# One long fp32 kernel: values and gates of each head pair as one 512-column product, input on the weights' queue, unread products at three waits, token scaling on GpSimd

## The reference, cut to what matters

```
# h_lat, h_ctx: 256 tokens each x 2048; 16 heads of 128
zf, zb, i, q, g = split(h_lat @ w_in, 5 x 2048)        # latent tokens: all five
zf_c, zb_c, i_c = split(h_ctx @ w_in[:, :6144], 3)     # context tokens: three
for each direction (forward with zf, backward with zb):
    f = lb + (1 - lb) * sigmoid(z);  k = (1 - lb) * sigmoid(-z)
    s_ctx = final state of k_c, v_c over the context, by chunks
    o    += chunked scan S_t = f_t S_(t-1) + k_t v_t, o_t = S_t q_t, from s_ctx
o = o * rsqrt(mean(o * o over 128) + eps)              # per token and head
y = (o * onorm_g * g * sigmoid(g)) @ w_out
```

## Time and profile before

| what | value |
| --- | --- |
| median of 3 runs | 3124.61 us |
| the profiled execution | 3124.67 us, of which the profile's span is 3122.9 |
| TensorE busy | 3083.2 us, 99% |
| VectorE, ScalarE, GpSimd busy | 64%, 46%, 3% |
| moved | 557.59 MB, mean 179 GB/s |
| one head pair of the recurrent mixer | some 99.7 us, eight of them |

### The profile page before, as it was taken

The page is one execution under the profiler, slowest core; times in us unless marked ns, Lnnn a source line. Parts: engine busy times, 40 slices in busy tenths (PEclk is TensorE's granted clock), DMA queues, the critical chain, the costliest instruction groups (busy, mean ns, idle before and its releaser), DMA issues.

```text
span 3122.9 us, 41500 instructions
## 1 busy us (share of the span) xinstructions
PE 3083.2 (99%) x16978; PEld 2666.3 (85%) x16978; DVE 1998.3 (64%) x2502; ACT 1422.3 (46%) x2029; POOL 97.3 (3%) x74
## 2 busy tenths in 40 slices
PE   8999999999999999999999999999999999999998
PEld 8989888888888888878888888888889999899987
DVE  6767777789888887857877755442743444443455
ACT  5344555465555554436422222232644544444454
POOL 0000003001111100000000000000000000000000
PEclk9999999999999999999999999999999999999999
DMA  8776666757667677775556555342333333333334
GB/s 302 231 248 216 208 212 216 250 179 230 213 221 225 216 251 266 254 240 197 161 170 191 178 193 179 127 150 95 103 96 104 100 108 114 102 110 97 112 131 146
DMA packets 369982, 557.59 MB, mean 179 GB/s; under 512 B 17088, under 2 KB 239296, under 8 KB 368512
## 3 DMA queue, kind: packets, MB, share of 16 engines
q1 hardware_dynamic: 366784, 540.08, 53.6%
q0 software_dynamic: 2000, 12.06, 1.0%
q10 hardware_dynamic: 1008, 2.80, 0.2%
HBM read 552.64 MB, written 2.23 MB: 178 GB/s over the span
## 4 chain that ended last, share of the span: by engine, by line
PE 95%; DVE 2%; ACT 1%; issue 1%; DMA 1%; ACTq 0%; DVEq 0%
PE ps L736 91%; DVE wlo L1746 1%; PE ps L933 0%; PE ps L948 0%; PE ps L938 0%; PE ps L950 0%; ACT whi L1152 0%; PE ps L807 0%; DMA CX<-in_ctx 0%; PE ps L771 0%; DVE HCl L1900 0%; PE ps L861 0%; PE ps L845 0%; PE ps L918 0%; PE ps L935 0%
## 5 line engine op out<-in xcount | busy, mean ns | idle before, releaser
L1746 DVE TENSOR_TENSOR wlo<-raw,whi 128x1024 fp32r<-128x1024 f32 (+1 forms) x823 | 1013.4, 1235 | 822.5 <-ACT whi L1152 820.6
L1152 ACT ACTIVATE whi<-raw 128x1024 fp32r<-128x1024 f32 x828 | 869.9, 1057 | 1166.5 <-PE ps L736 1150.3
L736 PE MATMUL ps<-HCh,whi 128*128 128x512 f32 (+1 forms) x1816 | 508.2, 361 | 0.0
L736 PE MATMUL ps<-HCh,wlo 128*128 128x512 f32 (+1 forms) x1816 | 500.8, 357 | 0.0
L736 PE MATMUL ps<-HCl,whi 128*128 128x512 f32 (+1 forms) x1816 | 500.3, 357 | 0.0
L736 PE MATMUL ps<-V,whi 128*128 128x512 f32 x1408 | 445.2, 398 | 0.8 <-DVE V L1902 0.8
L1763 DVE SCALAR_TENSOR_TENSOR acc<-raw_ada,S,acc 128x1024 f32<-128x1024 f32 x330 | 436.4, 1334 | 5.0 <-DMA raw_ada<-in_ada_w 4.2
L736 PEld LDWEIGHTS ps<-HCh,wlo 128*128 128x128 f32 x1816 | 323.6, 189 | 49.8
L736 PEld LDWEIGHTS ps<-HCl,whi 128*128 128x128 f32 x1816 | 323.5, 189 | 49.8
L736 PEld LDWEIGHTS ps<-HCh,whi 128*128 128x128 f32 x1816 | 319.7, 190 | 49.7 <-issue 4.2
L736 PEld LDWEIGHTS ps<-V,wlo 128*128 128x128 f32 x1408 | 265.4, 188 | 62.8
(11 more groups left out here) (345 smaller groups left out, 3484.5 us busy)
## 6 DMA issues: line engine op xcount, KB each, us to landing
raw_ada<-in_ada_w SPq DMA_DIRECT2D x192, 512.0 KB, 4.8
raw<-in_w_up SPq DMA_DIRECT2D x176, 512.0 KB, 4.3
raw<-in_w_in SPq DMA_DIRECT2D x160, 512.0 KB, 4.0
raw<-in_od_w_in SPq DMA_DIRECT2D x160, 512.0 KB, 3.5
raw<-in_ev_w_in SPq DMA_DIRECT2D x96, 512.0 KB, 3.8
raw<-in_w_down SPq DMA_DIRECT2D x88, 512.0 KB, 5.1
raw<-in_w_out SPq DMA_DIRECT2D x32, 512.0 KB, 4.8
raw<-in_w_ple_gate SPq DMA_DIRECT2D x32, 512.0 KB, 4.6
```

What stands on the lines that cost most here:

```text
L736: mm = e.matmul(o, a, b, start=first and t == 0, stop=last, skip_group_check=True)
L1152: e.activation(m.whi[ch.i % SPLIT][:, 0:n], m.raw[ch.slot][:, 0:n], ACT.Copy).then_inc(S("hi"), 1)
L1746: e.tensor_tensor(m.wlo[ch.i % SPLIT][:, 0:n], m.raw[ch.slot][:, 0:n], m.whi[ch.i % SPLIT][:, 0:n].bitcast(F32), ALU.subtract).then_inc(S( ...
```

## The change

- `schedule`: `v` and `g` of pairs 1 to 7 become one group `v` of 512 columns (`pair`), 2 k in a chunk, from a new array `od_w_vg` in which the columns of both lie side by side. TensorE's `values` multiplies the latent tokens with all 512 columns into the group's two banks and the context tokens with the 256 value columns into bank 6. The states `ds` of both heads move to bank 5.
- The order becomes q0 g0 v0 zf0 q1 zb0, then v zf q(j+1) zb; the last pair ends zf7 zb7. `g0` has tokens as rows. `hQ` and `hG` get two buffers each.
- `values` pumps twice in an even chunk and three times in an odd one, 20 in all; in `chunks` such a group pumps once in an even chunk and twice in an odd one.
- The readout: VectorE scales `OT` with the gate from `hG`, right behind the reciprocal; ScalarE makes `OH` from PSUM with `onorm`, VectorE `OL`. ScalarE takes the gate's sigmoids behind the copies of `hV`. `turn(0)` waits for `ol` instead of `og`.
- Start: `g_mix_pre` and `xt` are one array; its first part goes by ScalarE's queue, the other five by SyncE's after chunks 1 to 5 (`load_x`), `vec` and `cst` after chunk 7, `H` later. Chunk 0 comes and is split in two halves. ScalarE loads its table ahead of the input. U runs 1 k ahead.
- `hold`: 18 products of ones that nothing reads at the start and 18 behind `out3`, and 12 behind `ev3` after a wait for the banks of `ev2`.
- `tokens`: GpSimd scales the tokens of blocks 1 to 3 of X0 and X1.

```diff
-H_AT = (5, 6, 7, 8)
-ADA_FROM = 9
-XT_PARTS = ((0, 2), (2, 4), (4, 8), (8, 16))
+H_AT = (6, 8, 10, 11)
+ADA_FROM = 11
+XT_PARTS = ((0, 2), (2, 4), (4, 6), (6, 8), (8, 12), (12, 16))
...
+    def pair(self, name, W, j):
+
+        G = Group()
+        G.cols, G.K, G.kt, G.N, G.tm, G.raw, G.wide, G.first = 512, NT, 2, 2 * T, True, False, False, True
+        G.j0, G.j1, G.pair = 0, 8, True
+        G.s = self.sets % 2
+        self.sets += 1
+        G.use = self.uses[G.s]
+        self.uses[G.s] += 1
+        G.freed, G.base = G.use + 1, 2 * G.s
+        G.chunks = []
+        for i in range(8):
+            rows = W[i * 256:(i + 1) * 256, 512 * j:512 * j + 512]
+            G.chunks.append(self.stream(rows.rearrange("(k p) c -> p k c", p=128), 2, 512, True, True))
+        G.done = G.chunks[-1].n
+        self.by[name] = G
...
-        p.group(f"q{j}", W, 6144 + 256 * j, 256, NT, T)
         if j == 0:
-            p.group(f"g{j}", W, 8192 + 256 * j, 256, NT, T)
-        p.group(f"v{j}", W, 4096 + 256 * j, 256, NT, 2 * T, tm=True)
+            p.group("q0", W, 4096, 256, NT, T)
+            p.group("g0", A["od_w_vg"], 256, 256, NT, T, tm=True)
+            p.group("v0", A["od_w_vg"], 0, 256, NT, 2 * T, tm=True)
+        else:
+            p.pair(f"v{j}", A["od_w_vg"], j)
         p.group(f"zf{j}", W, 256 * j, 256, NT, 2 * T)
-        if j > 0:
-            p.group(f"g{j}", W, 8192 + 256 * j, 256, NT, T)
+        if j < 7:
+            p.group(f"q{j + 1}", W, 4096 + 256 * (j + 1), 256, NT, T)
         p.group(f"zb{j}", W, 2048 + 256 * j, 256, NT, 2 * T)
...
-        self.hQ = self.sb("hQ", [128, 2, T], F32, F + 28)
-        self.hG = self.sb("hG", [128, 2, T], F32, F + 30)
+        self.hQ = [self.sb(f"hQ{i}", [128, 2, T], F32, (F + 28, self.acc_at)[i]) for i in range(2)]
+        self.hG = [self.sb(f"hG{i}", [128, 2, T], F32, (F + 30, self.acc_at + 2)[i]) for i in range(2)]
...
+    def load_x(self, e, i):
+        k0, k1 = XT_PARTS[i]
+        c0, c1 = 16 + T * k0 if k0 else 0, 16 + T * k1
+        e.dma_start(self.gx[:, c0:c1], self.A["xt"][:, c0:c1]).then_inc(self.S(f"xt{i}"), 16)
...
-        return self.PS[5 + h][:, 128 * n:128 * n + 128]
+        return self.PS[5][:, 256 * h + 128 * n:256 * h + 128 * n + 128]
...
-            if self.serial and G.N == 512:
+            if self.serial and G.N == 512 and (j % 2 or not G.pair):
...
+        if ch.c == 0:
+            for k in range(2):
+                e.dma_start(dst[:, k, :], ch.src[:, k, :]).then_inc(S("raw0" if k else "raw_k0"), 16)
+        else:
+            e.dma_start(dst, ch.src).then_inc(S(f"raw{ch.slot}"), 16)
+        if 1 <= ch.c <= 5:
+            m.load_x(e, ch.c)
+        if ch.c == 7:
+            e.dma_start(m.vec[:, :], m.A["vec"]).then_inc(S("ld_vec"), 16)
+            e.dma_start(m.cst[:, :], m.A["cst"][:, 0:NCB]).then_inc(S("ld_cst"), 16)
...
+    def tokens(X, nm):
+        e.wait_ge(nm.s_rs, nm.n + 1)
+        for j in range(1, 4):
+            e.wait_ge(X.s_p, X.n_p + 4 * (j - 1))
+            for b in range(2):
+                t = e.tensor_scalar(X.hn[:, j % 2, b, :], m.H[:, b, 512 * j:512 * j + 512], nm.rs[:, b:b + 1], None,
+                                    ALU.mult)
+            t.then_inc(X.s_m, 1)
...
+    def values(self, j, X):
+
+        m, S, e = self.m, self.S, self.e
+        G = self.plan.by[f"v{j}"]
+        e.wait_ge(S(f"set{G.s}"), G.use)
+        if j > 1:
+            old = self.plan.by[f"v{j - 1}"]
+            e.wait_ge(S(f"set{old.s}"), old.freed)
+        for i, ch in enumerate(G.chunks):
+            self.pump()
+            e.wait_ge(S("lo_dve"), ch.n_lo)
+            ws = [w[ch.i % SPLIT][:, :].rearrange("p (k c) -> p k c", k=2) for w in (m.whi, m.wlo)]
+            for k in range(2):
+                kk = 2 * i + k
+                if k:
+                    self.pump()
+                for t in range(3):
+                    for b in range(2):
+                        e.matmul(m.PS[G.base + b][:, :], (X.lo if t == 1 else X.hi)(kk)[:, 128 * b:128 * b + 128],
+                                 ws[t == 2][:, k, :], start=kk == t == 0, stop=kk == NT - 1 and t == 2,
+                                 skip_group_check=True)
+                if i % 2 and not k:
+                    self.pump()
+                for t in range(3):
+                    for b in range(2):
+                        mm = e.matmul(m.PS[6][:, 256 * b:256 * b + 256],
+                                      (X.lo if t == 1 else X.hi)(kk)[:, T + 128 * b:T + 128 * b + 128],
+                                      ws[t == 2][:, k, 0:256], start=kk == t == b == 0,
+                                      stop=kk == NT - 1 and t == 2, skip_group_check=True)
+            mm.then_inc(S("mm"), 1)
+
+    def hold(self, bank, n):
...
+        for _ in range(n):
+            self.e.matmul(m.PS[bank][:, 0:128], m.ones[:, :], m.ones[:, :], start=True, stop=True,
+                          skip_group_check=True)
...
-            if X.scaled:
+            if X.split and k:
+                e.wait_ge(X.s_m, X.n_m + k // 4)
...
-                e.wait_ge(S("og"), j)
+                e.wait_ge(S("ol"), j)
...
+    e.wait_ge(S("init"), 3)
+    P.hold(4, 18)
...
     for g in range(4):
         P.group(f"out{g}", X)
+    P.hold(7, 18)
...
+    G = plan.by["ev2"]
+    e.wait_ge(S(f"set{G.s}"), G.freed)
+    P.hold(7, 12)
...
+            P.group("v0", X)
+        else:
+            P.values(j, X)
...
-        if j:
-            P.group(f"g{j}", XQ)
+        if j < 7:
+            P.group(f"q{j + 1}", XQ)
...
+            if ch.c == 0:
+                e.wait_ge(S("raw_k0"), 16)
+                e.activation(m.whi[0][:, 0:512], m.raw[0][:, 0:512], ACT.Copy).then_inc(S("hi_k0"), 1)
+                e.wait_ge(S("raw0"), 16)
+                e.activation(m.whi[0][:, 512:1024], m.raw[0][:, 512:1024], ACT.Copy).then_inc(S("hi"), 1)
+                continue
...
-        e.wait_ge(S("ri"), j + 1)
-        for i in range(4):
-            a = e.activation(m.OT[:, i, :], m.PS[7][:, 128 * i:128 * i + 128], ACT.Copy, scale=m.SM[:, 4 + i:5 + i])
-        a.then_inc(S("ot"), 1)
-        yield
-        e.wait_ge(S("og"), j + 1)
-        e.activation(m.OH[:, 2 * j:2 * j + 2, :], m.hG[:, :, :], ACT.Copy).then_inc(S("oh"), 1)
+        yield
+        e.wait_ge(S("otr"), j + 1)
+        for h in range(2):
+            a = e.activation(m.OH[:, 2 * j + h, :], m.PS[4][:, 256 * h:256 * h + 256], ACT.Copy,
+                             scale=m.v("onorm", 2 * j + h))
+        a.then_inc(S("oh"), 1)
...
-    e.dma_start(m.v("g_mix_pre", 0, 16), m.A["vec"][:, VEC["g_mix_pre"]:VEC["g_mix_pre"] + 16]).then_inc(S("ld_g"), 16)
-    for i, (k0, k1) in enumerate(XT_PARTS):
-        e.dma_start(m.xt[:, k0:k1, :], m.A["xt"][:, k0:k1, :]).then_inc(S(f"xt{i}"), 16)
-    e.dma_start(m.vec[:, 16:NVEC], m.A["vec"][:, 16:NVEC]).then_inc(S("ld_vec"), 16)
-    e.dma_start(m.cst[:, :], m.A["cst"][:, 0:NCB]).then_inc(S("ld_cst"), 16)
-    e.wait_ge(S("ld_g"), 16)
+    m.load_x(e, 0)
+    e.wait_ge(S("init"), 3)
+    e.activation(m.SM[:, 24:25], m.ones[:, 0:1], ACT.Copy)
...
+        if j > 1:
+            e.wait_ge(S("qd"), 2 * j - 2)
+        e.activation(m.hQ[j % 2][:, :, :], PS[G.base][:, :], ACT.Copy).then_inc(S(f"set{G.s}"), 1)
...
+            for b in range(2):
+                e.activation(m.hV[:, b, :], PS[G.base + b][:, 0:256], ACT.Copy)
+            e.activation(m.hV[:, 2:4, :], PS[6][:, :], ACT.Copy)
+            if j > 1:
+                e.wait_ge(S("ol"), j - 1)
+            for b in range(2):
+                a = e.activation(m.hG[j % 2][:, b, :], PS[G.base + b][:, 256:512], ACT.Sigmoid)
+            a.then_inc(S("gs"), 1)
...
+            if ch.c == 0:
+                for c, hi, lo in ((0, "hi_k0", "lo_k0"), (512, "hi", "lo_dve")):
+                    e.wait_ge(S(hi), 1)
+                    e.tensor_tensor(m.wlo[0][:, c:c + 512], m.raw[0][:, c:c + 512],
+                                    m.whi[0][:, c:c + 512].bitcast(F32), ALU.subtract).then_inc(S(lo), 1)
...
-            if k % 4:
+            if k % 4 or X.split and k:
...
-        yield
-        yield
-        yield
-        e.wait_ge(S("otr"), j + 1)
-        G = self.plan.by[f"g{j}"]
+        e.wait_ge(S("ri"), j + 1)
+        G = self.plan.by[f"v{j}" if j else "g0"]
         e.wait_ge(S(f"set{G.s}"), G.freed)
+        for i in range(4):
+            h, p = divmod(i, 2)
+            t = e.scalar_tensor_tensor(m.OT[:, i, :], m.PS[7][:, 128 * i:128 * i + 128], m.SM[:, 4 + i:5 + i],
+                                       m.hG[j % 2][:, p, 128 * h:128 * h + 128], ALU.mult, ALU.mult)
+        t.then_inc(S("ot"), 1)
+        yield
+        yield
+        yield
+        e.wait_ge(S("oh"), j + 1)
         for h in range(2):
-            t = e.scalar_tensor_tensor(m.hG[:, h, :], m.PS[4][:, 256 * h:256 * h + 256], m.v("onorm", 2 * j + h),
-                                       m.hG[:, h, :], ALU.mult, ALU.mult)
-        t.then_inc(S("og"), 1)
```

(68 more changed lines are left out.)

69 lines of the change are left out of this document (35 added, 34 removed).

## The result

The changed kernel takes 3157.3 us, the median of 4 runs (3155.97 to 3158.85), against 3124.73 before: a ratio of 1.0104, 95% interval 1.0091 to 1.0116. The profiled execution spans 3153.9 us, 31.0 more than the one before.

What follows compares the result with a forecast made beforehand. TensorE, busy 3083 of 3123 us, was taken as the bound, so only its products and waits count. Terms from -7.3 (joined products) to +20.3 and +13.3 (new waits) summed to +20.5: 3145, range 3108 to 3155, likeliest case 3132 to 3155.

Steps and rivals of the forecast that it cites:

- The waits: Joined groups: TensorE waits 2.9 us at `turn(0)` and 1.9 at `turn(1)`, seven times each: +20.3 and +13.3 us.
- The time of `kd`, T + 17.5: Joined groups: `kd` stays ready 17.5 us after T, the end of `zb`; TensorE asks at T + 14.7.
- The rival that the helpers keep pace: Joined groups: `kd` at T + 12.7 and an early mask remove the 33.6 and 2.1 us: 3109; chance 0.22.
- The start: Kernel start: first real product at 7.0 to 8.0 us instead of 10.96; -4.8 us in all (-2 to -6.5).
- The half pace: Start: first 16 products take 3.4 us at half pace; unread products take over the lost 1.6 us.
- Unread products behind `out3`: Second stage wait: 18 products keep the clock up but outlast the wait by 0.9 us; net -0.5 (-2 to +1).
- The third wait: Third stage wait: VectorE loses three pairs of scalings (2.7 us) to GpSimd: -1.8 us.
- rival 3: GpSimd is late at 2.34 us per operation, each of six requests some 0.9 us late, +5.4: 3150; chance 0.08.
- The products: Joined values and gates, v1 to v7: wider products save 0.065 us a k, 7.3 us over 16 k and 7 groups.
- The readout's +2.1: Readout: four scalings of `OT` end 0.3 us after TensorE asks, seven times: +2.1 us (0 to 5).
- The waits around `zf7` and `zb7`: Last pair: 0.5 at `turn(0)`, 1.7 for `kdT`, 1.3 at `outputs(1)`, less 1.1 for `hA`: +2.4 us.
- rival 4: Start: no gain, since the input queued with the weights lands no earlier: 3149; chance 0.05.

Runs made afterwards that it cites:

- the first experiment: Changed kernel with ScalarE and VectorE taking two steps in each of the first four chunks of a joined group, one in the last four: 3115.89 us, ratio 0.9972.
- the kernel with the waits filled: Changed kernel with 12 unread products ahead of TensorE's wait for the decayed keys (`turn(0)`) in each joined group: 3149.95 us, ratio 1.0079.
- the keys-first kernel: Changed kernel with two steps on ScalarE and VectorE in chunks 0, 1, 5 and 7 of a joined group: 3129.72 us, ratio 1.0015.

## Why the prediction was wrong in size

**The direction and its cause were right.** The waits were named with their places, 2.9 and 1.9 us; they are 2.76 (1.85 in the first group) and 1.77. The time of `kd`, T + 17.5, is met to 0.1 us. The rival that the helpers keep pace failed for the reason given against it: its order needs two steps in the first chunks. With them (the first experiment) `kd` ends at T + 12.7 and the kernel takes 3115.9, where the rival said 3109; 4.6 of these 6.9 us are the start and the stages up to `zf0`, forecast at -7.6 and measured at -3.0.

**The failed step is the price of a wait.** The sum took 2.9 us of waiting for 2.9 us of time, "So TensorE waits 17.6 - 14.7 = 2.9 us at `turn(0)`, seven times: 20.3 us", and added nothing for what TensorE does behind it. Yet the same text read in the earlier trace rows that the clock falls behind waits of 2.8 and 1.9 us, and used it only for the old waits. Five falls of 1.55 (7.8) and a restart of 0.36 a group (2.5) are 10.3 us, against a miss of 10.5 in the whole. That the two are so near is chance: the parts outside the mixer came out 4.6 worse than forecast, and the mixer's other terms 4.4 better, 1.9 of it because the first group waited 1.85 us and the others 2.76. The fall in the trace and the kernel with the waits filled show the 7.8; the restart is what is left of a stretch beside both waits and was not tried by itself.

**The start** was taken too well by 2.7 us. The first real product came at 7.24, inside 7.0 to 8.0 (held up by the unread products, not by its data), but the forecast let the rest of U arrive in time. The change from three k ahead to one was in the diff and got no price. It made two waits of 2.3 us in all; with three k ahead they shrink to 0.4, and 0.9 us comes back. The half pace, 1.6 in the sum, is hidden here: leaving the 18 products out costs at most 0.4. What else keeps the start from -4.8 stays open.

**Unread products behind `out3`.** The 0.9 us by which they outlast the wait was right (0.8); of the 1.4 us that the clock was to give back 0.7 came (15.9 us for the transposes instead of 16.6). VectorE bounds that stretch, which the prediction said and then did not follow far enough.

**The third wait** was forecast at -1.8 by way of GpSimd's scalings (2.7 us less for VectorE). The trace gives -1.0. Of X1's gain 1.5 us come and go with the clock, between kernels that are the same there. GpSimd was slower than said, 1.83 and 1.90 us (median of the instructions at X0 and X1, 1.55 to 2.90) instead of 1.3 to 1.4. Yet no wait of TensorE ends at a GpSimd instruction, so rival 3 did not come true; the 0.5 us for `hnf` ends at VectorE (L2005). At X1:

```profile
L641 POOL TENSOR_SCALAR hnf<-H,SN x6: 1552/1900/2898, 2209.1 to 2221.7; 128x512 f32<-128x512 f32 x6
```

The Trainium skill, page "SBUF — State Buffer", section "SBUF: two separate sides", would have a GpSimd instruction stand still beside certain VectorE ones; the spread from 1.55 to 2.90 agrees, without showing the cause.

**Small terms.** The products give 0.06 us a k, not 0.065. By the Trainium skill's fixed cost of a matmul (page "TensorE: Matmul & The Clock Gate", section "Wait — 56ns, not 53.3ns?") six products fewer would give 0.015; the trace gives four times that, 10 ns each, and the measurement decides. The readout's +2.1 is 0.7: no wait stands at its transposes. No wait names the double buffers. The waits around `zf7` and `zb7` are 0.4, 1.6 and 1.3 us, where 0.5, 1.7 and 1.3 were forecast. Two sums of the prediction are off by one: without the start's gain rival 4 comes to 3150, and its period of a head pair to 103.8 by its own terms; 103.7 is what the groups without a fall have.

**The range** ended at 3155, 2.3 us short. Its upper bound took the longer waits and again no clock.

## What to carry to other kernels

When work beside a product stream runs in steps, a change of the stream's groups moves when each step is asked for; write down, for each engine, which split or copy stands ahead of the step that the next engine waits for, and count the steps to that point. Price a new wait in TensorE's stream at its length plus what the clock costs behind it, read from the nearest wait of the same length in the trace, and test it with unread products in the wait's place. Before a larger product is given up because the kernel became slower, try it with the steps in another order.

## What was not expected of the hardware

A wait of 2.76 us cost the clock in five of six otherwise equal places and not in the sixth of the same execution. One of 1.77 us cost it in none of 14 (the keys-first kernel and the one with the first wait filled), the one of 1.85 us did not, and one of 1.98 us at X1 in six of ten executions. Each fall took some 1.5 us from work that had not changed. The changed kernel's runs spread over 2.9 us and those of the kernel before over 0.6, which would fit two falls more or less (3.1 us). That is not shown: only one execution has a trace, and the runs of the first experiment's kernel, whose trace has no fall in a joined group, spread over 3.1 us as well.
